# Two-layer decoder on one core: three output pieces' low parts move to GpSimd, a shorter index mask, and the first attention unit at other places in its engines' order

## The reference, cut to what matters

```python
def _token_mixer(x, w_in, ...):            # fox: 4 heads, nsa: 6 query heads, dsa: 6 heads
    p = _split_columns(x @ w_in)
    o_fox = _fox_attention(...)            # softmax(q k / 8 + bias) v
    o_nsa = _nsa_attention(...)            # compressed, selected and windowed branches
    o_dsa = _dsa_attention(...)            # keys kept by an indexer's top 64, else NEG
    o = concatenate([o_fox, o_nsa, o_dsa])
    return o @ w_out
for l in range(2):
    x = layer_norm(ALPHA * x + _token_mixer(x, ...))
    x = layer_norm(ALPHA * x + moe(x, ...))    # 64 experts, 8 a token, and one shared
```

## Time and profile before

| what | value |
|---|---|
| three runs | 1241.19, 1241.99, 1243.54 us (median 1241.99) |
| the profiled execution | 1243.89 us, of which its span in the trace is 1242.1 us |
| PE busy | 1209.8 us (97%) |
| DVE, ACT, GpSimd busy | 555.9, 340.2, 122.9 us |
| mean granted clock of PE | 0.996 |

### The profile page before, as it was taken

One profiled execution on the slowest core, in us unless ns is written; L12 is line 12 of the kernel. 1 busy time (PEld: TensorE's weight loads), 2 busy tenths in 40 slices (PEclk: granted clock), 3 DMA queues, 4 the chain that ended last, 5 costly groups with the idle time before them and its releaser, 6 DMA issues.

```text
span 1242.1 us, 25211 instructions
## 1 busy us (share of the span) xinstructions
PE 1209.8 (97%) x10381; PEld 631.4 (51%) x10383; DVE 555.9 (45%) x1550; ACT 340.2 (27%) x701; POOL 122.9 (10%) x173
## 2 busy tenths in 40 slices
PE   9998999999999999999999989999999999999995
PEld 7885754334344443433398858433433444443341
DVE  4788553333333333333468877433333333333334
ACT  4667321111111111111265574111111111111111
POOL 2662110000000000000035421000000000000000
PEclk9999999999999999999999999999999999999998
DMA  9444799999999999999945529999999999999994
GB/s 356 166 178 206 281 399 427 425 426 427 425 425 424 429 426 426 426 426 426 385 149 190 222 99 360 389 427 426 425 428 425 427 424 427 425 427 426 425 427 189
DMA packets 42425, 454.88 MB, mean 366 GB/s; under 512 B 4944, under 2 KB 5712, under 8 KB 8016
## 3 DMA queue, kind: packets, MB, share of 16 engines
q1 hardware_dynamic: 42032, 452.27, 87.6%
q10 hardware_dynamic: 288, 1.05, 0.2%
HBM read 452.26 MB, written 1.05 MB: 365 GB/s over the span
## 4 chain that ended last, share of the span: by engine, by line
PE 79%; DVE 11%; DMA 6%; ACT 2%; issue 2%; DVEq 0%; POOL 0%; ACTq 0%; POOLq 0%
PE banks L1050 33%; PE banks L1070 17%; PE banks L1026 7%; PE banks L1081 5%; DMA expert_weights<-in_moe_w 5%; PE banks L1058 2%; PE banks L970 1%; PE banks L917 1%; DVE prob L1685 1%; PE banks L918 1%; PE banks L919 1%; PE banks L633 1%; PE banks L1007 1%; PE banks L601 1%; DVE sm_neg L1668 1%
## 5 line engine op out<-in xcount | busy, mean ns | idle before, releaser
L1050 PE MATMUL banks<-expert_weights,gathered 128*64 128x512 f32 x1520 | 339.8, 595 | 1.4 <-DMA expert_weights<-in_moe_w 1.4
L1050 PEld LDWEIGHTS banks<-expert_weights,gathered 128*64 128x64 f32 x1520 | 105.6, 137 | 230.7 <-issue 230.7
L1070 PE MATMUL banks<-expert_weights,hT 128*32 128x512 f32 x1600 | 182.0, 595 | 2.5 <-DVE hT L1892 2.5
L1887 DVE TENSOR_TENSOR sig<-sig,banks 128x256 f32<-128x256 f32 x64 | 27.0, 421 | 338.9 <-ACT sig L1422 338.6
L1435 ACT ACTIVATE y_hi<-banks,gate_slot 128x512 fp32r<-128x512 f32 x126 | 86.6, 687 | 295.1 <-PE banks L1070 295.1
L1897 DVE SCALAR_TENSOR_TENSOR y_lo<-banks,gate_slot,y_hi 128x512 fp32r<-128x512 f32 x126 | 94.6, 751 | 157.4 <-ACT y_hi L1435 157.4
L1422 ACT ACTIVATE sig<-banks 128x256 f32<-128x256 f32 x64 | 24.6, 384 | 407.8 <-PE banks L1050 407.8
L1026 PEld LDWEIGHTS banks<-hot,x_part 128*128 128x128 bf16 x3072 | 93.3, 98 | 48.7 <-issue 48.7
L1070 PEld LDWEIGHTS banks<-expert_weights,hT 128*32 128x32 f32 x1600 | 47.2, 109 | 109.7 <-issue 108.2
L1026 PE MATMUL banks<-hot,x_part 128*128 128x64 bf16 x3072 | 100.7, 193 | 0.0
L1491 POOL TENSOR_TENSOR piece_lo<-piece,piece_hi 128x256 fp32r<-128x256 f32 x112 | 87.8, 819 | 80.3 <-ACT piece_hi L1247 65.2
(11 more groups left out here) (244 smaller groups left out, 1526.0 us busy)
## 6 DMA issues: line engine op xcount, KB each, us to landing
expert_weights<-in_moe_w SPq DMA_DIRECT2D x132, 2048.0 KB, 23.2
expert_weights_in_ring<-in_moe_w SPq DMA_DIRECT2D x20, 2048.0 KB, 23.3
piece<-in_pieces SPq DMA_DIRECT2D x32, 1024.0 KB, 5.0
expert_weights<-in_moe_w SPq DMA_DIRECT2D x26, 1024.0 KB, 8.2
expert_weights_in_rows<-in_moe_w SPq DMA_DIRECT2D x22, 1024.0 KB, 22.5
expert_weights_in_x<-in_moe_w SPq DMA_DIRECT2D x22, 1024.0 KB, 23.3
expert_weights_in_ring<-in_moe_w SPq DMA_DIRECT2D x8, 1024.0 KB, 7.8
shared_weights<-in_ws SPq DMA_DIRECT2D x2, 3072.0 KB, 12.8
```

Of the source, the lines that this page charges most:

```text
L1050: mm = pe.matmul(C[e * PAIR:(e + 1) * PAIR, :], xgT[:, d, e * PAIR:(e + 1) * PAIR], w[e][:, part], start=(d == 0), stop=(d == KD - 1))
L1070: mm = pe.matmul((A, B)[c][to:to + SLOTS, :], hT[:, f, of_:of_ + SLOTS], W[QUARTERS + c][e][:, f * 512:(f + 1) * 512], start=(f == 0), sto ...
```

## The change

Four edits.
- The low parts of pieces 14, 15 and 16 are made by GpSimd, behind `vc_blocks`; the rounding of piece 16 as well, in eight copies. DVE's five instructions and ACT's two halves for them go.
- `index_mask` has five instructions of 128 columns that write `dmask` directly, instead of four of which two had 384.
- DVE's `maxima(0)` stands inside `index_top`, before its sixth round of 256 columns; `normalise(0)` stands right behind `index_top`, ahead of `rotate(7, (0,))`.
- On ACT a one-column exponential stands ahead of `exps(0)`, and `split_hi(11)` behind it.

```diff
--- before.py
+++ after.py
-LO_VECTOR = (2, 3, 6, 14, 15, 16)
+LO_VECTOR = (2, 3, 6)
 LO_POOL = [n for n in SPLIT if n not in LO_VECTOR]
+MAXIMA_AMID = 5
...
-        dmask_ready = sem("dsa_mask_ready", 1)
+        dmask_ready = sem("dsa_mask_ready", 3)
...
-                    def split_last_hi(half):
-                        n, cols = SPLIT_OUT[3], slice(half * SLOT // 8, (half + 1) * SLOT // 8)
-                        act.wait_ge(*at(piece_ld[n % RING], piece_count(n)))
-                        hi_free(act, n)
-                        own.mark(act.copy(flat_piece(hi_of(n))[:, cols], flat_piece(piece[n % RING])[:, cols]))
-                        if half:
-                            own.settle()
-                            act.nop().then_inc(hi_ready, 1)
...
                     read_plain(6)
-                    split_hi(11)
+                    act.activation(ln_s[:, 0, 22:23], own_number[:, 0:1], ACT.Exp, scale=-1.0)
...
                     exps(0)
+                    split_hi(11)
                     split_hi(12)
...
                     probs_out(4)
-                    split_last_hi(0)
                     read_turned(10)
...
                         heads_out(v - 1)
-                        if v == 6:
-                            split_last_hi(1)
...
-                    for n in LO_POOL:
-                        if n == LO_POOL[-2]:
+                    for n in LO_POOL[:-3]:
+                        if n == LO_POOL[-5]:
                             pool.wait_ge(*at(p_ready, 2))
+                        rounded_by_scalar(n)
                         split_lo(n)
                     pool.wait_ge(*at(kv_sb, 2))
                     if layer == 0:
-                        pool.wait_ge(heads_known, 1)
+                        pool.wait_ge(masks_ready, 1)
...
+                    for n in SPLIT_OUT[1:3]:
+                        rounded_by_scalar(n)
+                        split_lo(n)
+                    n = SPLIT_OUT[3]
+                    pool.wait_ge(*at(piece_ld[n % RING], piece_count(n)))
+                    hi_free(pool, n)
+                    for k in range(KD):
+                        own.mark(G.tensor_copy(hi_of(n)[:, k, :], piece[n % RING][:, k, :]))
+                    own.settle()
+                    split_lo(n)
                     pool.wait_ge(*at(proj, 2 * N_IN_PIECES))
...
-                            for _ in range(TOPK // 8):
+                            for i in range(TOPK // 8):
+                                if a and i == MAXIMA_AMID:
+                                    maxima(0)
...
                     def index_mask():
-                        own.link(V.tensor_scalar(score[:, :], score[:, :], -2.0e38, NEG, ALU.is_gt, ALU.mult))
                         for a in (0, 2 * P):
-                            own.mark(V.tensor_tensor(score[:, a:a + P], score[:, a:a + P], cmask[:, 0, :], ALU.add))
+                            own.mark(V.tensor_scalar(score[:, a:a + P], score[:, a:a + P], -2.0e38, NEG, ALU.is_gt, ALU.mult))
+                        V.tensor_scalar(dmask[:, P:2 * P], score[:, P:2 * P], -2.0e38, NEG, ALU.is_gt, ALU.mult).then_inc(dmask_ready, 1)
                         own.settle()
-                        V.tensor_copy(dmask[:, :], score[:, :]).then_inc(dmask_ready, 1)
+                        for a in (0, 2 * P):
+                            V.tensor_tensor(dmask[:, a:a + P], score[:, a:a + P], cmask[:, 0, :], ALU.min).then_inc(dmask_ready, 1)
...
                     index_top()
-                    maxima(0)
+                    normalise(0)
                     rotate(7, (0,))
-                    normalise(0)
...
                     index_mask()
-                    split_lo(14)
                     rotate(9, (0,))
...
-                        if 5 <= u < 9:
-                            split_out(2 + (u - 5) // 2, (u - 5) % 2)
-                        if u in (6, 8):
-                            own.settle()
-                            dve.nop().then_inc(lo_dve, 1)
```

More of the change, by code:

```diff
@@ L295, in build @@
         still_ready, once, rope_ld, x_ld, rows_ld, stored, masks_ready = alone("zeros_ready"), alone("constants_loaded"), alone("rope_loaded"), [alone(f"x_turned_half{g}_loaded") for g in range(2)], alone("x_loaded"), alone("output_stored"), alone("masks_ready")
-        heads_known = alone("own_heads_known")
         first_piece = [sem(f"first_piece_half{g}_loaded", 16) for g in range(2)]
@@ L352, in build @@
         xhi_ready, xlo_ready = sem("x_hi_ready", 2), sem("x_lo_ready", 2)
-        hi_ready, lo_dve, lo_pool = sem("piece_hi_ready", len(SPLIT)), sem("piece_lo_by_vector", len(LO_VECTOR)), sem("piece_lo_by_gpsimd", len(LO_POOL))
+        hi_ready, lo_dve, lo_pool = sem("piece_hi_ready", len(SPLIT) - 1), sem("piece_lo_by_vector", len(LO_VECTOR)), sem("piece_lo_by_gpsimd", len(LO_POOL))
         heads_split = sem("heads_split", KD)
@@ L745, in scores @@
                         if kind == "dsa":
-                            pe.wait_ge(*at(dmask_ready, 1))
+                            pe.wait_ge(*at(dmask_ready, 3))
                         tq, tk = {"fox": (T_FQ + i, T_FK + i), "slc": (T_NQ + i, T_KS), "win": (T_NQ + i, T_KW), "dsa": (T_DQ + i, T_DK)}[kind]
@@ L1488, in split_lo @@
                     def split_lo(n):
-                        pool.wait_ge(*at(hi_ready, SPLIT.index(n) + 1))
                         for k in range(KD):
@@ L1494, in split_lo, with rounded_by_scalar @@
                         pool.nop().then_inc(lo_pool, 1)
-                    for n in LO_POOL:
-                        if n == LO_POOL[-2]:
+                    def rounded_by_scalar(n):
+                        pool.wait_ge(*at(hi_ready, SPLIT.index(n) + 1))
+                    for n in LO_POOL[:-3]:
+                        if n == LO_POOL[-5]:
                             pool.wait_ge(*at(p_ready, 2))
+                        rounded_by_scalar(n)
                         split_lo(n)
@@ L1649, in _ @@
                         dve.wait_ge(once, 16 * 4)
-                        V.tensor_reduce(own_head[:, :], ident[:, :].rearrange("p (h c) -> p h c", c=16), AX, ALU.add).then_inc(heads_known, 1)
+                        own.mark(V.tensor_reduce(own_head[:, :], ident[:, :].rearrange("p (h c) -> p h c", c=16), AX, ALU.add))
                         own.mark(V.tensor_copy(identb[:, :], ident[:, :]))
@@ L1736, in cmp_norm @@
                         V.tensor_tensor(rows_, rows_, pcs[:, 2, :].unsqueeze(2).broadcast_to([P, TT * heads, NC]), ALU.mult).then_inc(pc_ready, 1)
-                    def split_out(i, half):
-                        n, cols = SPLIT_OUT[i], slice(half * SLOT // 8, (half + 1) * SLOT // 8)
-                        dve.wait_ge(*at(hi_ready, SPLIT.index(n) + 1))
-                        own.mark(V.tensor_tensor(flat_piece(piece_lo[n % RING])[:, cols], flat_piece(piece[n % RING])[:, cols],
-                                                 flat_piece(hi_of(n)).bitcast(F32)[:, cols], ALU.subtract))
                     normalise(2)
```

## The result

The changed kernel took 1245.60 us (median of 18 runs, 1244.67 to 1248.79); the kernel before, run beside it, 1242.47 (18 runs). The ratio is 1.0026, 95% interval 1.0019 to 1.0032: slower, by 3.1 us. The forecast was 1239.3, with 1244.0 as its upper end. The profiled execution of after took 1245.19 us, its span is 1243.3. That is only 1.2 above the span of before, whose profiled execution lay 1.4 above its own median, so the two traces show less than the whole difference.

The account below looks back on a forecast made before the run. PE's own work bounds the kernel, DVE its attention tail. First unit 0.4, index mask and piece 14 1.5, tail 0.8: 2.7 us off the 1241.99 median gives 1239.3 us, range 1235.8 to 1244.0.

Parts of the forecast that it names:

- The lead: DVE 4 us ahead at the first rotary step of column group 9, 1.7 from the mask, 2.3 from piece 14.
- PE's lead of 1.9 us: PE enters the tail 1.9 us earlier over both layers: 0.4 from the first unit, 1.5 from rotary steps.
- The mask: Index mask on DVE: five instructions take 1.2 us (bounds 0.9 and 2.9) instead of 2.90.
- The first unit: Attention stage, layer 0: PE no longer waits at unit 1's scores, 0.4 us won; nothing in layer 1.
- The delay of piece 11's rounding is covered: First unit, ACT: the later rounding costs nothing, since PE needs that piece only some 10 us later.
- The tail: Units 5 to 8 win 1.6 us a layer, GpSimd waits ahead cost 1.2; 0.4 a layer, 0.8 in all.
- GpSimd at no cost of its own: GpSimd finishes four pairs of heads at 119.1 us, PE asks at about 120.5; margin 1.4 us, cost 0.
- transfers that follow PE: Layer 1's last load: the weight stream's long part comes as much earlier as PE does, so the gain stays.
- DVE waits for whole instructions of GpSimd: Rival: first meeting costs half of a 0.69 us GpSimd instruction, later ones all; 4.1 us slower, 1246.1 us; chance 0.05.
- given back: Rival: DVE waits 0.49 us each time, the tail loses 2.0 us a layer; 1244.1 us at far end; chance 0.25.
- GpSimd costs nearly nothing: Rival: DVE hardly waits for GpSimd, the tail gives 2.3 us a layer; 6.5 us faster, 1235.5 us; chance 0.20.

Follow-up runs that it names:

- e7: Changed kernel, but GpSimd sets the low parts of pieces 14 to 16 to zero without reads, so the output lacks them; ratio 0.9970 to the kernel before.
- e3: Kernel before with only the shorter index mask; ratio 1.0008 to the kernel before.
- e4: Kernel before with only the first unit's new order, its exponentials ahead of piece 11's rounding; ratio 1.0025 to the kernel before.
- e5: Kernel before with the first unit's maxima amid the index rounds and its division early, piece 11's rounding still ahead of the exponentials; ratio 1.0000.
- e6: Changed kernel with ACT's rounding of piece 11 ahead of the first exponentials; ratio 1.0035 to the kernel before.
- e9: Changed kernel with matmuls of zeros ahead of unit 6's scores and unit 5's division, nothing reading their output; ratio 1.0022 to the kernel before.
- e12: Kernel before with 0.43 us of zero matmuls ahead of PE's wait for the rotary step of column group 9; ratio 1.0002.
- e13: Changed kernel with GpSimd's low parts of pieces 14 to 16 in sixteen instructions of 128 columns instead of eight of 256; ratio 1.0096 to the kernel before.
- e14: Changed kernel with GpSimd's low parts of pieces 14 to 16 in thirty-two instructions of 64 columns each; ratio 1.0173 to the kernel before.
- e17: Changed kernel with low parts of pieces 14 and 15 in sixteen instructions, GpSimd holding piece 14 until DVE's compressed-branch subtraction is done; ratio 1.0004 to kernel before.
- e15: Changed kernel with GpSimd's low parts of pieces 14 to 16 in one instruction of 2048 columns each; ratio 1.0100 to the kernel before.
- e2: Kernel before with only the move of pieces 14 to 16 to GpSimd; ratio 1.0057 to the kernel before.
- e8: Kernel before with only piece 16's rounding and low part moved to GpSimd, 14 and 15 staying on DVE; ratio 1.0029.
- e10: Kernel before with piece 16 alone moved, plus zero matmuls ahead of unit 6's scores and the divisions of units 5 and 6; ratio 1.0039.

## Why the prediction was wrong

**The step that failed** is the one behind the tail's gain: "Against it, the divisions of units 2 to 4 and two products of the compressed branch, which met no GpSimd before, now do: 11 instructions, 3.6 us, of which DVE's new lead and its waits for PE hide, by my estimate, two thirds." Both halves were too kind. The price was 0.51 us for each product in a division, not 0.33. I had averaged between rows with a piece running and a row with a pair of heads, but a DVE that works without a pause meets every instruction of a GpSimd that works without a pause. By the rows from 88 to 106 us, two sums, two divisions, the short products and unit 4's division cost some 4.2 us more (0.9 + 2.05 + 0.9 + 0.3), against the 3.6 of the sum. The cover was the larger error. The prediction hid 2.4 us of 3.6; DVE waited for PE and ACT for about 1 us in that stretch of before, no more, so PE entered the tail 3.1 us later. The lead was missing too: at the first rotary step of column group 9 DVE is 1.0 us ahead of before (83.37 against 84.39), where the prediction had 4, since the mask gave nothing of its 1.7 and DVE came to the mask 1.3 us late (80.58 against 79.28). The sum had this stretch at 1.2 lost a layer, and with PE's lead at 0.3.

**PE's lead of 1.9 us** over both layers was the second error. The rotary step did come in time, by piece 14's 2.3 us and not by the mask. But e7, without GpSimd's reads, shows what such a lead is worth: PE has its scores of unit 6 at 101.81 us, 0.7 ahead of before, and then waits 1.57 us for exponentials in place of 0.80. It enters the tail at 105.72, against 105.93. So 0.2 us of the lead is left. A chain through the last projection, a rotary step, the division of unit 4, and the maxima and exponentials of unit 5 stood right behind the wait that was removed.

**The mask** was sized at 1.2 us from two sums without GpSimd; all five instructions meet GpSimd and take 2.8. e3 confirms that it wins nothing.

**The first unit**: its wait went, 0.4 us. "The delay of piece 11's rounding is covered" looked only at PE's need for the piece. GpSimd's work on it moved by 4 us onto DVE's short operations; alone that costs 1.0025 (e4) against 1.0000 (e5). In the changed kernel it hides behind the other loss (e6).

**The tail** was right in kind, and in size partly by luck: 1.6 us a layer forecast, 2.0 measured (20.75 to 18.8). The sum had GpSimd beside all of units 5 to 8 at 0.33 a product. In fact the products of units 5 and 6 waited 0.51 and 0.3 each, and those of units 7 and 8 not at all, because GpSimd is done with its pieces at 113.1 us. GpSimd at no cost of its own, and transfers that follow PE, were right too. In layer 1 the clean comparison is e9 against e12, which have no stretch at half clock there: 104.2 us against 101.1 from the layer's start to the scores of unit 7, 18.8 against 20.8 in the tail. Twice 3.1 lost less 2.0 won is 2.2 us. Of the other 0.9 us some 0.5 may be clock (e9), which the intervals don't separate from none.

**The rivals.** The third error is their order. "DVE waits for whole instructions of GpSimd" had 0.05 and gave 1246.1. The measured 1245.6 is next to it, and e13, e14 and e17 show its mechanism, but that the numbers meet is chance: it had the tail lose 0.9 us a layer and 2.1 lost ahead of it, where 2.0 were won and 3.1 lost. By price, 0.49 a wait, "given back" was nearer (0.51 measured); it too hid two thirds ahead of the tail, and gave 1244.1. I had held the mask's 0.49 a sum against its 0.69. But a wait for the rest of an instruction of 0.7 is itself about 0.5: the row did not speak against that rival. The Trainium skill ("SBUF — State Buffer", section "Who interferes with whom") says that the engine that issues first holds the shared ports for the whole instruction; the divisions at 2.05, 1.51 and 1.23 us agree. By the same section `tensor_scalar` can contend in its faster mode: here it took 0.64 us against 0.22, and which mode it ran in no run shows. "GpSimd costs nearly nothing" gave 1235.5; e7 measured 1238.75 for it, with piece 11 still late and with GpSimd's pieces shorter as well.

## What to carry to other kernels

Work that leaves a busy engine for one that shares its way to memory is paid in waits at each instruction, and here they were nearly as long as the other engine's instructions (0.51 of 0.73 us): count every instruction of the busy engine in the new stretch at the full price, and hide only as much as its idle time in the rows. Before counting a removed wait as a lead, look for the next thing that the same engine would wait for; the chain of waits of a kernel so tight changes its engine within a microsecond or two. Short instructions on the helper together with a wait that keeps it off one chained operation gave back here about what the move had cost, and no more; short instructions alone (e13) cost 8.7 us more than the move.

## What was not expected of the hardware

- One DVE instruction with two operands in SBUF stood still for 4.5, 7.3 and 9.1 us, through six to about thirty GpSimd instructions that followed each other without a gap, while others got their turn between two of them. In the changed kernel the same subtraction, begun at the same point of `vc_blocks`, got through in 0.77 us. What decides it is open; it came in both layers of e13 to e15 (PE's wait in layer 1 of e13: 5.67 us) and in one of e2.
- `tensor_scalar` on one operand in SBUF waits too (0.64 in place of 0.22 us), the maxima from PSUM and the rotary products that read PSUM do not (1.02 and 0.42 throughout).
- The same low part, with DVE standing still, takes GpSimd 4.54 us in one instruction, 5.55 in eight, 6.66 in sixteen and 9.02 in thirty-two.
- PE's waits of 1.35 and 1.44 us in the changed kernel's tail were followed by a stretch at half clock in layer 1 and by none in layer 0. Where PE waited for DVE anyway, half clock cost little or nothing: nothing in e8's tail against e10's, and in the changed kernel's layer 1 some 0.7 of 1.7 us (19.6 us of tail against e9's 18.8).
